# A causal pooling mixer reordered: group matrix product ahead of the token averages, averages as a banded matrix on TensorE

## The chip, the cores and the metric

The kernel runs on one core of a Trainium2 chip. The metric is the device time of one execution in microseconds; of several runs the median stands. A profile is of one execution.

## What is computed

The model has two layers on a stream x of 256 tokens by 2048 features, all in float32. Layer 0 mixes tokens by causal averages (the pooling mixer), layer 1 by latent attention; each is followed by a SwiGLU feed-forward part. The change is in the pooling mixer, the first thing the kernel does.

```python
def multiscale_pool_mixer(h, pool_w, pool_scale):      # h = rms_norm(x, pool_norm)
    cs = jnp.cumsum(hf, axis=1)
    for g, w in enumerate((2, 4, 8, 16)):              # a window for each group of 512 features
        c = cs[..., sl]
        c_prev = jnp.pad(c, ((0, 0), (w, 0), (0, 0)))[:, :S]
        count = jnp.minimum(t + 1, w)
        diff = (c - c_prev) / count - hf[..., sl]      # mean of the last w tokens, less the token itself
        outs.append(diff @ pool_w[g])                  # 512x512 matrix of the group
    return jnp.concatenate(outs, axis=-1) * pool_scale
x = x + multiscale_pool_mixer(rms_norm(x, pool_norm), pool_w, pool_scale)
x = x + (silu(h @ w_gate) * (h @ w_up)) @ w_down       # h = rms_norm(x, ffn_norm)
```

## The kernel before

Features lie on the 128 partitions, tokens along the free dimension: `x` is 16 tiles of 128x256, and tiles 4g to 4g+3 are group g. The engines run programs of their own and meet at semaphores; every order below is written out by hand.

**SyncE** issues all loads in one queue (`load`, L298 to L304): the four quarters of x (512 KB each), gains, constants, positions, and then eight chunks of `pool_w` of 512 KB into the eight slots of `raw`. After these come the chunks of the feed-forward weights (`up0`, ...), each as soon as the chunk that held its slot has been used.

**The pooling stage.** ScalarE squares the quarters of x into `x_square` (L710), VectorE adds them up (L1061, L1062), TensorE sums over the partitions with a matrix of ones (L424), ScalarE takes the root (L695) and VectorE the reciprocal (L1025, 128x256). ScalarE has meanwhile put x times the gain into `normed` (L715). VectorE multiplies by the reciprocal (L1072), makes the window sums of groups 0, 1 and 2 by shifted additions (L1080), corrects the first tokens (L1089) and writes mean less token into `pooled` (L1090). GpSimd does the multiplication of groups 1 to 3 (L1457) and the window sums of group 3 (L1448). TensorE then multiplies in float32 (`pool_tile`, L435): for each of 16 output tiles four matmuls with a 128x128 block of `raw` as the stationary operand and 256 columns of `pooled` as the moving one. The profile shows a float32 matmul as two records. VectorE adds the product to x (`pool_out`, L1099).

**The hand-over.** Each finished tile of x goes through `gained`: ScalarE writes the rounded product with the next gain (L701), VectorE the rest (L1031), side by side in `xg` as float32r. ScalarE also squares the tile (L724), and GpSimd adds it to `square_sum` (L1509). The first four weight chunks of `up0` are split in the same manner, high part by ScalarE (L689), low part by GpSimd (L1502); all later low parts are VectorE's (L1021).

**The feed-forward part** starts with `first_tiles`: two output tiles side by side, over tiles 0 to 7 of `xg` with chunks 0 and 1, then over tiles 8 to 15 with chunks 2 and 3. A product is a pair: `w_hi` on 512 columns (L373) and `w_lo` on 256 columns (L374). Then comes `sum_over_partitions` (L414) and the rest of the kernel, which the change leaves as it is.

## Time and profile before

| | |
|---|---|
| median of 3 runs | 1820.53 us (1820.5 to 1821.93) |
| span of the profiled execution, first to last instruction | 1818.9 us |
| TensorE busy | 1774.5 us, 98% |
| VectorE busy | 1163.2 us, 64% |
| ScalarE busy | 921.5 us, 51% |
| GpSimd busy | 188.2 us, 10% |
| first matmul of the feed-forward part starts | 67.44 us |
| `sum_over_partitions` after `first_tiles` starts | 78.62 us |

Of the profiled execution only the span is on record; the median of the runs is 1.6 us above it. Times within the trace count from the start of the span. PE is TensorE, PEld its loads of the stationary operand, DVE VectorE, ACT ScalarE, POOL GpSimd, SP SyncE. "ps" is the accumulator memory (PSUM), eight banks of 512 columns. Rows that name L701 and L724 (ScalarE) are a tile's hand-over.

### The profile page before, as it was taken

The numbers are of one execution on the slowest core, as the hardware profiler recorded it, in microseconds if no ns is written. First come the engines' busy times: TensorE is split into PE (matmuls) and PEld (weight loads), VectorE is DVE, ScalarE is ACT, GpSimd is POOL, SyncE is SP. The second block draws the span as 40 slices with busy tenths as digits, with TensorE's granted clock in tenths as the row PEclk, the third lists the DMA queues.
The fourth block names the chain that finished last, engine by engine and source line by source line (L and its number), as shares of the span: only waits on it lengthen the run. The fifth ranks groups of instructions, "written<-read, shape, count | busy, mean of one in ns | idle before, by whom it ended". The sixth has DMA issues, their size and how long they took to land.

```text
span 1818.9 us, 29323 instructions
## 1 busy us (share of the span) xinstructions
PE 1774.5 (98%) x10300; PEld 1571.6 (86%) x10300; DVE 1163.2 (64%) x1427; ACT 921.5 (51%) x1195; POOL 188.2 (10%) x198
## 2 busy tenths in 40 slices
PE   6899999999999999999999999999999999999997
PEld 5788888888888888888888888888888888888886
DVE  7766666556666666668777776666655566666554
ACT  3565655333445454456776456556533344445442
POOL 5400000000000001124322430000000000000112
PEclk8999999999999999999999999999999999999998
DMA  4555556654555565544334556555655455556541
GB/s 180 172 196 189 184 188 230 201 177 153 192 187 190 190 231 192 178 150 134 122 127 139 195 175 197 192 188 190 229 198 181 150 188 192 186 192 225 194 162 46
DMA packets 83998, 326.64 MB, mean 180 GB/s; under 512 B 9456, under 2 KB 9712, under 8 KB 83952
## 3 DMA queue, kind: packets, MB, share of 16 engines
q1 hardware_dynamic: 83952, 326.04, 54.2%
q8 instruction: 27, 0.44, 0.1%
q14 instruction: 19, 0.16, 0.0%
HBM read 323.91 MB, written 2.10 MB: 179 GB/s over the span
## 4 chain that ended last, share of the span: by engine, by line
PE 90%; DVE 5%; ACT 3%; issue 2%; POOL 0%; DMA 0%; DVEq 0%; SPq 0%; ACTq 0%; POOLq 0%
PE ps L373 57%; PE ps L374 30%; ACT w_hi L689 1%; DVE win_v L1080 1%; ACT product L845 1%; PE ps L435 0%; DVE xg L1031 0%; DVE w_lo L1021 0%; DMA x<-xT 0%; PE ps L527 0%; DVE prob L1355 0%; PE ps L526 0%; PE ps L525 0%; DVE pooled L1090 0%; ACT prob L905 0%
## 5 line engine op out<-in xcount | busy, mean ns | idle before, releaser
L1021 DVE TENSOR_TENSOR w_lo<-raw,w_hi 128x1024 fp32r<-128x1024 f32 (+2 forms) x557 | 731.3, 1315 | 422.6 <-ACT w_hi L689 422.1
L373 PE MATMUL ps<-xg,w_hi 128*128 128x512 f32 x2880 | 999.4, 390 | 1.0 <-POOL w_lo L1502 1.0
L689 ACT ACTIVATE w_hi<-raw 128x1024 fp32r<-128x1024 f32 (+2 forms) x562 | 630.2, 1124 | 494.5 <-PE ps L374 494.5
L374 PE MATMUL ps<-xg,w_lo 128*128 128x256 f32 x2880 | 812.2, 282 | 0.0
L373 PEld LDWEIGHTS ps<-xg,w_hi 128*128 128x128 f32 x2880 | 540.4, 188 | 114.7 <-POOL w_lo L1502 1.4
L374 PEld LDWEIGHTS ps<-xg,w_lo 128*128 128x128 f32 x2880 | 544.3, 189 | 0.1
L373 PE MATMUL ps<-act,w_hi 128*128 128x512 f32 x1408 | 488.3, 390 | 0.0
L374 PE MATMUL ps<-act,w_lo 128*128 128x256 f32 x1408 | 397.1, 282 | 0.0
L373 PEld LDWEIGHTS ps<-act,w_hi 128*128 128x128 f32 x1408 | 264.2, 188 | 55.4
L374 PEld LDWEIGHTS ps<-act,w_lo 128*128 128x128 f32 x1408 | 266.1, 189 | 0.0
L1467 POOL TENSOR_TENSOR square<-x 128x256 f32 (+1 forms) x47 | 42.4, 903 | 1452.0 <-DVE x L1151 1452.0
L1130 DVE TENSOR_TENSOR sums<-ps,cross 128x512 f32<-128x512 f32 x88 | 60.9, 692 | 95.6 <-ACT cross L734 95.6
L734 ACT ACTIVATE cross<-ps 128x512 f32<-128x512 f32 x88 | 52.6, 598 | 120.6 <-PE ps L374 120.5
L373 PE MATMUL ps<-heads,w_hi 128*128 128x512 f32 x256 | 89.1, 391 | 0.0
L1150 DVE TENSOR_TENSOR x<-ps,x 128x256 f32 (+1 forms) x80 | 33.8, 422 | 66.4 <-PE ps L374 66.4
L701 ACT ACTIVATE xg<-x,gain 128x256 fp32r<-128x256 f32 (+1 forms) x48 | 24.4, 508 | 100.4 <-DVE x L1151 62.1
L374 PE MATMUL ps<-heads,w_lo 128*128 128x256 f32 x256 | 72.2, 282 | 0.0
L1134 DVE TENSOR_TENSOR sums<-sums,rstd 128x512 f32<-128x512 f32 x88 | 60.9, 692 | 3.0
L737 ACT ACTIVATE gate_act<-sums 128x256 f32<-128x256 f32 x88 | 36.8, 418 | 46.0 <-DVE sums L1134 45.7
L373 PE MATMUL ps<-latent,w_hi 128*128 128x512 f32 x160 | 56.9, 395 | 0.6 <-DVE sums L1300 0.6
L373 PEld LDWEIGHTS ps<-heads,w_hi 128*128 128x128 f32 x256 | 48.1, 188 | 10.0
L1031 DVE SCALAR_TENSOR_TENSOR xg<-x,gain,xg 128x256 fp32r<-128x256 f32 (+1 forms) x48 | 39.4, 832 | 19.9 <-ACT xg L701 19.8
(168 smaller groups left out, 1202.5 us busy)
## 6 DMA issues: line engine op xcount, KB each, us to landing
raw<-w_gate SPq DMA_DIRECT2D x176, 512.0 KB, 3.5
raw<-w_up SPq DMA_DIRECT2D x176, 512.0 KB, 3.3
raw<-w_down SPq DMA_DIRECT2D x128, 704.0 KB, 4.1
raw<-w_o SPq DMA_DIRECT2D x32, 512.0 KB, 3.3
raw<-pool_w SPq DMA_DIRECT2D x8, 512.0 KB, 11.0
raw<-w_q_a SPq DMA_DIRECT2D x8, 512.0 KB, 3.3
raw<-w_kv_a SPq DMA_DIRECT2D x8, 512.0 KB, 3.3
raw<-w_q_nope SPq DMA_DIRECT2D x8, 512.0 KB, 3.3
```

Source lines behind the costliest of these rows:

```text
L373: pe.matmul(ps[:, bank, :], w_hi[:, s, j * P:(j + 1) * P], moving, start=start, stop=False)
L374: return pe.matmul(ps[:, bank, 0:SEQ], w_lo[:, s, j * P:(j + 1) * P], moving[:, 0:SEQ], start=False, stop=stop)
L689: nc.scalar.activation(dst, src, ACT.Copy).then_inc(hi_ready, 1)
L701: nc.scalar.activation(dst[:, plus(t, i, per), 0:SEQ], x[:, plus(t, i, per), :], ACT.Identity, scale=gain[:, plus(col + t, i, per), :]).th ...
L734: nc.scalar.activation(cross[:, :, :], ps[:, bank:bank + 2, SEQ:], ACT.Copy).then_inc(cross_ready, 1)
L737: nc.scalar.activation(gate_act[:, :], sums[:, 0, :], ACT.Silu).then_inc(gate_ready, 1)
L1021: nc.vector.tensor_tensor(lo, src, hi.bitcast(F32), ALU.subtract).then_inc(lo_ready, 1)
L1031: nc.vector.scalar_tensor_tensor(dst[:, plus(t, i, per), SEQ:], x[:, plus(t, i, per), :], gain[:, plus(col + t, i, per), :], dst[:, plus(t ...
L1130: nc.vector.tensor_tensor(sums[:, :, :], ps[:, bank:bank + 2, 0:SEQ], cross[:, :, :], ALU.add).then_inc(evacuated, 2)
L1134: nc.vector.tensor_tensor(sums[:, :, :], sums[:, :, :], r, ALU.mult).then_inc(sums_ready, 1)
L1150: step(nc.vector.tensor_tensor(xd, ps[:, b, 0:SEQ], xd, ALU.add))
L1467: step(nc.gpsimd.tensor_tensor(square[:, :], src, src, ALU.mult))
```

## The change

- TensorE multiplies by the group's matrix first (`pool_product`): the stationary operand is a block of `x_pool`, which is x times the gain with tokens as its 128 columns, the moving operand 512 columns of `raw`, in float32. The result has tokens on the partitions, 512 features of the group along the free dimension, in banks 4 to 7. A chunk of `pool_w` now holds half of a group's rows.
- The norm is applied to that result: a token is a partition there, so `tok_rstd` is a column of 128 for each half of the tokens. Squares are summed by `token_squares`, two columns wide; root and reciprocal are 128x2.
- ScalarE writes the scaled result rounded (`product_hi`), VectorE the rest (`product_lo`) into `z`, float32r.
- The averages are a banded 256x256 matrix for each window, made on the host and loaded as `bands` (128 partitions x 4 x 272 numbers, 544 KB). GpSimd brings it to float32r (`band`). `mix` multiplies `z` as the stationary operand by it: five matmuls a tile, of 256, 144, 16, 128 and 128 columns. The last group's `mix` stands in the middle of `first_tiles`.
- `pool_out` reads what `mix` left, and goes on with `gained` tile by tile or group by group. The low parts of the first four chunks of `up0` are VectorE's now.
- The loads are reordered: gains and `pool_w` chunks go between the quarters of x. The window sums, their corrections and buffers are gone, as are 18 matmuls of warm-up after the sum of squares; the first warm-up has 10 instead of 8. GpSimd's first fills have a 128x1600 one for `band` among them, for which the warm-up waits.

```diff
-WARM_UP = 8
-WARM_UP_POOL = 18
+WARM_UP = 10
...
+SPILL = P + PAD
+BAND_IN = SPILL + P
+B_FIRST, B_SECOND, B_LOW, B_COLS = 0, SEQ, SEQ + P, SEQ + P + PAD
...
+        z = at("z", [P, 2, 2, 2, GT * P], F32R, pool_at)
+        x_pool = at("x_pool", [P, DT, SEQ], F32, pool_at + 16 * KB)
+        band_in = at("band_in", [P, GROUPS, BAND_IN], F32, pool_at + 32 * KB)
+        band = at("band", [P, GROUPS, B_COLS], F32R, pool_at + 38 * KB)
+        tok_root = at("tok_root", [P, 2, 1], F32, scratch_at)
+        tok_rstd = at("tok_rstd", [P, 2, 1], F32, scratch_at + 64)
...
+        def mix_bank(t):
+            return t % GT if t < DT - GT else GT + t % GT
...
+            load_x(0)
+            sp.dma_start(gain[:, :, :], gains).then_inc(gain_landed, 16)
+            load(0, pool_w[0])
+            load_x(1)
+            load_x(2)
+            load(1, pool_w[1])
+            load_x(3)
+            load(2, pool_w[2])
+            sp.dma_start(band_in[:, :, :], bands).then_inc(band_landed, 16)
+            for c in range(3, 2 * GROUPS):
+                load(c, pool_w[c])
...
-                        bank_free(t + m)
+                        if t == TILE["up0"]:
+                            pe.wait_ge(evacuated, t + m - 7)
+                        else:
+                            bank_free(t + m)
...
-            for _ in range(WARM_UP_POOL):
-                pe.matmul(ps[:, SCORES, 0:P], ones[:, :], ones[:, :], start=True, stop=True)
...
+            def pool_product(g, half):
+                c = 2 * g + half
+                pe.wait_ge(landed[c], 16)
+                for s in range(2):
+                    if half == 0 and g >= 2:
+                        pe.wait_ge(z_ready, 2 * (g - 2) + s + 1)
+                    for j in range(2):
+                        kt = 2 * half + j
+                        if s == 0:
+                            pe.wait_ge(pool_gained, GT * g + kt + 1)
+                        mm = pe.matmul(ps[:, 4 + 2 * (g % 2) + s, :], x_pool[:, GT * g + kt, s * P:(s + 1) * P],
+                                       raw[:, c, j * GT * P:(j + 1) * GT * P], start=(kt == 0), stop=(kt == GT - 1))
+                mm.then_inc(chunks_used, 1)
+            def token_squares():
+                pe.wait_ge(quarter_ready, 4)
+                for s in range(2):
+                    mm = pe.matmul(ps[:, s, 0:2], x_square[:, DT - GT, s * P:(s + 1) * P], ones[:, 0:2],
+                                   start=True, stop=True)
+                mm.then_inc(stats_summed, 1)
+            def mix(g):
+                pe.wait_ge(z_ready, 2 * g + 2)
+                for j in range(GT):
+                    t = GT * g + j
+                    if 4 <= t < 12:
+                        pe.wait_ge(evacuated, t - 3)
+                    bank = mix_bank(t)
+                    first_hi, first_lo = (z[:, g % 2, 0, part, j * P:(j + 1) * P] for part in range(2))
+                    second_hi, second_lo = (z[:, g % 2, 1, part, j * P:(j + 1) * P] for part in range(2))
+                    pe.matmul(ps[:, bank, 0:SEQ], first_hi, band[:, g, B_FIRST:B_FIRST + SEQ], start=True, stop=False)
+                    pe.matmul(ps[:, bank, 0:SPILL], first_lo, band[:, g, B_FIRST:B_FIRST + SPILL], start=False,
+                              stop=False)
+                    pe.matmul(ps[:, bank, 0:PAD], first_hi, band[:, g, B_LOW:B_LOW + PAD], start=False, stop=False)
+                    pe.matmul(ps[:, bank, P:SEQ], second_hi, band[:, g, B_SECOND:B_SECOND + P], start=False,
+                              stop=False)
+                    pe.matmul(ps[:, bank, P:SEQ], second_lo, band[:, g, B_SECOND:B_SECOND + P], start=False,
+                              stop=True).then_inc(mixed, 1)
+            pool_product(0, 0)
+            pool_product(0, 1)
+            pool_product(1, 0)
+            token_squares()
+            pool_product(1, 1)
+            pe.wait_ge(band_ready, 3)
+            mix(0)
+            pool_product(2, 0)
+            pool_product(2, 1)
+            mix(1)
+            pool_product(3, 0)
+            pool_product(3, 1)
+            mix(2)
...
+                    if layer == 0:
+                        first_tiles(n0, t0, xg_before, (0,))
+                        mix(GROUPS - 1)
+                        first_tiles(n0, t0, xg_before, (1,))
+                    else:
+                        first_tiles(n0, t0, xg_before)
...
+            def product_hi(g):
+                sc.wait_ge(chunks_used, 2 * g + 2)
+                if g >= 2:
+                    sc.wait_ge(mixed, GT * (g - 1))
+                for s in range(2):
+                    nc.scalar.activation(z[:, g % 2, s, 0, :], ps[:, 4 + 2 * (g % 2) + s, :], ACT.Identity,
+                                         scale=tok_rstd[:, s, :]).then_inc(z_hi, 1)
...
+            def pooled_tile(t):
...
+            sc.wait_ge(gain_landed, 16)
+            pool_gain(0)
+            quarter_square(0)
+            pool_gain(1)
+            quarter_square(1)
+            quarter_square(2)
+            quarter_square(3)
+            pool_gain(2)
+            sc.wait_ge(stats_summed, 1)
+            nc.scalar.activation(tok_root[:, :, :], ps[:, 0:2, 0:1], ACT.Sqrt, bias=eps[:, :],
+                                 scale=1.0 / D_MODEL).then_inc(root_ready, 1)
+            sc.wait_ge(rstd_ready, 1)
+            product_hi(0)
+            pool_gain(3)
+            product_hi(1)
+            for t in range(4):
+                pooled_tile(t)
+            split(CHUNK["up0"])
+            product_hi(2)
+            for t in range(4, 8):
+                pooled_tile(t)
+            split(CHUNK["up0"] + 1)
+            product_hi(3)
+            for t in range(8, 12):
+                pooled_tile(t)
+            split(CHUNK["up0"] + 2)
+            split(CHUNK["up0"] + 3)
+            for t in range(12, DT):
+                pooled_tile(t)
...
-                nc.vector.tensor_tensor(c, c, x_square[:, 4 * q + 1, :], ALU.add).then_inc(quarter_ready, 1)
-            ve.wait_ge(init_ready, INIT)
-            ve.wait_ge(const_landed, 16)
+                ins = nc.vector.tensor_tensor(c, c, x_square[:, 4 * q + 1, :], ALU.add)
+                if q >= 1:
+                    step(ins)
+                    ins = nc.vector.tensor_tensor(c, c, x_square[:, 4 * q - 4, :], ALU.add)
+                ins.then_inc(quarter_ready, 1)
+                ve.wait_ge(quarter_ready, q + 1)
...
-            def pool_out(*tiles):
-                for t in tiles:
-                    if t % 2 == 0:
-                        ve.wait_ge(chunks_used, t // 2 + 1)
-                    nc.vector.scalar_tensor_tensor(x[:, t, :], ps[:, t % 4, 0:SEQ], gain[:, G_SCALE + t, :],
-                                                   x[:, t, :], ALU.mult, ALU.add).then_inc(evacuated, 1)
-            for a in (0, GT // 2):
-                b = a + GT // 2
-                norm_tiles(a, b, b)
-                pool_diff(0, window_sums(0, a, b), a // (GT // 2) + 1, a, b)
-            ve.wait_ge(normed_ready, 1)
-            pool_diff(1, window_sums(1), 3)
-            pool_out(0, 1, 2, 3)
-            ve.wait_ge(normed_ready, 2)
-            win = window_sums(2)
-            pool_out(4, 5)
-            pool_diff(2, win, 4)
-            pool_out(6, 7)
-            ve.wait_ge(windows_ready, 1)
-            pool_diff(3, win_p2, 5)
-            for t in range(DT // 2):
-                gained(t, G_FFN0, xg, t + 1)
-            for t in range(DT // 2, DT):
+            ve.wait_ge(root_ready, 1)
+            nc.vector.reciprocal(tok_rstd[:, :, :], tok_root[:, :, :]).then_inc(rstd_ready, 1)
+            ve.wait_ge(rstd_ready, 1)
+            def product_lo(g):
+                for s in range(2):
+                    ve.wait_ge(z_hi, 2 * g + s + 1)
+                    nc.vector.scalar_tensor_tensor(
+                        z[:, g % 2, s, 1, :], ps[:, 4 + 2 * (g % 2) + s, :], tok_rstd[:, s, :],
+                        z[:, g % 2, s, 0, :].bitcast(F32), ALU.mult, ALU.subtract).then_inc(z_ready, 1)
+            def pool_out(t):
+                ve.wait_ge(mixed, t + 1)
+                nc.vector.scalar_tensor_tensor(x[:, t, :], ps[:, mix_bank(t), 0:SEQ], gain[:, G_SCALE + t, :],
+                                               x[:, t, :], ALU.mult, ALU.add).then_inc(evacuated, 1)
+            product_lo(0)
+            product_lo(1)
...
+            for g in range(GROUPS - 1):
+                for t in range(GT * g, GT * g + GT):
+                    pool_out(t)
+                for t in range(GT * g, GT * g + GT):
+                    gained(t, G_FFN0, xg, t + 1)
+                split(CHUNK["up0"] + g)
+                if g < 2:
+                    product_lo(g + 2)
+            split(CHUNK["up0"] + GROUPS - 1)
+            for t in range(DT - GT, DT):
                 pool_out(t)
                 gained(t, G_FFN0, xg, t + 1)
-            ve.wait_ge(lo_ready, SPLIT_SLOTS)
...
+            for ap, value in ((ones[:, :], 1.0), (eps[:, :], EPS), (band[:, :, :].bitcast(F32), 0.0),
+                              (stat[:, :, :], 0.0)):
...
+            gp.wait_ge(band_landed, 16)
+            nc.gpsimd.tensor_copy(band[:, :, B_FIRST:B_FIRST + SPILL], band_in[:, :, 0:SPILL]).then_inc(band_ready, 1)
+            nc.gpsimd.tensor_copy(band[:, :, B_SECOND:B_SECOND + P], band_in[:, :, SPILL:]).then_inc(band_ready, 1)
+            gp.wait_ge(band_ready, 2)
+            nc.gpsimd.tensor_tensor(band[:, :, B_LOW:B_LOW + PAD], band_in[:, :, 0:PAD],
+                                    band[:, :, B_FIRST:B_FIRST + PAD].bitcast(F32), ALU.subtract).then_inc(band_ready, 1)
...
-                if t in FIRST_SPLITS:
-                    split(CHUNK["up0"] + FIRST_SPLITS.index(t))
...
+def pool_bands():
+    s, t = np.arange(P)[:, None], np.arange(SPILL)[None, :]
+    out = np.zeros((P, GROUPS, BAND_IN), np.float32)
+    for g, w in enumerate(WINDOWS):
+        seen, own = (t >= s) & (t < s + w), (t == s).astype(np.float32)
+        out[:, g, 0:SPILL] = np.where(seen, 1.0 / np.minimum(t + 1.0, w), 0.0) - own
+        out[:, g, SPILL:] = (np.where(seen, 1.0 / w, 0.0) - own)[:, 0:P]
+    return out
...
-        "pool_w": np.concatenate([by_tiles(w, GT, 2) for w in a["pool_w"][0]]),
+        "pool_w": a["pool_w"][0].reshape(2 * GROUPS, 2, P, GT * P).transpose(0, 2, 1, 3).reshape(2 * GROUPS, P, -1),
```

## Rows read from the trace of the kernel before

**Rows 1.** The page: the span and the busy time of each engine.
```profile
span 1818.9 us, 29323 instructions
...
PE 1774.5 (98%) x10300; PEld 1571.6 (86%) x10300; DVE 1163.2 (64%) x1427; ACT 921.5 (51%) x1195; POOL 188.2 (10%) x198
```

**Rows 2.** Windows: length, PE, PEld, DVE, ACT, POOL busy, PE's clock, DMA share, GB/s.
```profile
0.00:67.44 67.44, 47.02 (x188) 38.05 (x189) 54.23 (x53) 25.43 (x52) 41.32 (x36) 0.90 0.43 155
...
78.78:1818.90 1740.12, 1716.17 (x10048) 1523.52 (x10047) 1102.25 (x1364) 889.89 (x1133) 143.81 (x158) 1.00 0.55 180
```

**Rows 3.** The chain that ended last, 0 to 82 us: start, length, what.
```profile
13.58 1.76 DVE rstd L1025
...
37.74 8.85 PE ps L435 x32
...
66.68 0.77 issue
```

**Rows 4.** Timeline of PE: start, length, what, records.
```profile
1.66 3.79 PE L421 MATMUL ps<-ones 128*128 128x128 f32 x16 [1.66 <-POOL stat L1444]
...
37.74 15.74 PE L435 MATMUL ps<-pooled,raw 128*128 128x256 f32 x64 [2.96 <-DVE x L1099]
...
67.87 0.39 PE L373 MATMUL ps<-xg,w_hi 128*128 128x512 f32 x1
...
78.62 0.59 PE L414 MATMUL ps<-square_sum,ones 128*128 128x256 f32 x2
```

**Rows 5.** Windows in the pooling stage (columns as in rows 2).
```profile
23.90:27.50 3.60, 3.57 (x8) 2.86 (x9) 3.56 (x2) 0.00 (x0) 3.52 (x2) 0.50 0.00 0
27.50:29.50 2.00, 1.94 (x9) 1.38 (x7) 1.97 (x2) 0.00 (x0) 1.92 (x2) 0.98 0.00 0
```

**Rows 6.** Timeline of PE in the attention part, float32r matmuls back to back.
```profile
960.73 0.28 PE L596 MATMUL ps<-probT,v_buf 128*128 128x256 f32 x1
960.85 0.22 PE L594 MATMUL ps<-probT,v_buf 128*128 128x128 f32 x1
960.91 0.28 PE L595 MATMUL ps<-probT,v_buf 128*128 128x128 f32 x1
961.02 0.27 PE L596 MATMUL ps<-probT,v_buf 128*128 128x128 f32 x1
```

**Rows 7.** Timeline of POOL: fills, and one addition of the window sums.
```profile
0.74 0.20 POOL L1444 MEMSET ones<- 128x128 f32 x1 [0.29 <-POOLq L1623]
...
0.92 0.31 POOL L1444 MEMSET normed<- 128x256 f32 x1
...
23.40 2.22 POOL L1448 TENSOR_TENSOR win_p<-normed 128x1024 f32<-128x1024 f32 x1
```

**Rows 8.** Timeline of ACT at the start of the kernel.
```profile
5.11 1.06 ACT L710 ACTIVATE x_square<-x 128x1024 f32<-128x1024 f32 x1 [2.87 <-DMA x<-xT]
6.38 1.06 ACT L710 ACTIVATE x_square<-x 128x1024 f32<-128x1024 f32 x1 [0.22 <-DMA x<-xT]
...
13.35 4.88 ACT L715 ACTIVATE normed<-x,gain 128x256 f32<-128x256 f32 x12
```

**Rows 9.** Timeline of DVE.
```profile
10.51 0.69 DVE L1061 TENSOR_TENSOR x_square<-x_square 128x512 f32<-128x512 f32 x1
...
26.21 2.27 DVE L1080 TENSOR_TENSOR win_v<-normed 128x512 f32<-128x512 f32 x1
...
66.87 0.47 DVE L1099 SCALAR_TENSOR_TENSOR x<-ps,gain,x 128x256 f32<-128x256 f32 x1
...
68.33 0.47 DVE L1099 SCALAR_TENSOR_TENSOR x<-ps,gain,x 128x256 f32<-128x256 f32 x1
```

**Rows 10.** The page's groups: line, operation, count, busy, mean ns, idle before.
```profile
L1021 DVE TENSOR_TENSOR w_lo<-raw,w_hi 128x1024 fp32r<-128x1024 f32 (+2 forms) x557 | 731.3, 1315 | 422.6 <-ACT w_hi L689 422.1
...
L689 ACT ACTIVATE w_hi<-raw 128x1024 fp32r<-128x1024 f32 (+2 forms) x562 | 630.2, 1124 | 494.5 <-PE ps L374 494.5
...
L734 ACT ACTIVATE cross<-ps 128x512 f32<-128x512 f32 x88 | 52.6, 598 | 120.6 <-PE ps L374 120.5
```

More of the change, by code:

```diff
@@ L133, in plus, with trunk @@
     return n if i is None else i * per + n
-def trunk(nc, xT, positions, consts, gains, pool_w, w_kv_a, w_k_pe, w_q_a, w_kv_k, w_kv_v, w_q_nope, w_q_pe,
+def trunk(nc, xT, positions, consts, bands, gains, pool_w, w_kv_a, w_k_pe, w_q_a, w_kv_k, w_kv_v, w_q_nope, w_q_pe,
           w_o, w_gate, w_up, w_down, out):
@@ L246, in trunk @@
         init_ready = sem("init_ready")
-        windows_ready = sem("windows_ready")
-        normed_ready = sem("normed_ready")
-        diff_ready = sem("diff_ready")
+        band_landed = sem("band_landed")
+        band_ready = sem("band_ready")
+        z_hi = sem("z_hi")
+        z_ready = sem("z_ready")
+        mixed = sem("mixed")
         angle_ready = sem("angle_ready")
@@ L289, in trunk @@
         KV, Q = 0, 1
-        INIT = 8
+        INIT = 4
         UPS = ("up0", "up1", "up2", "up3")
@@ L304, in load, with load_x @@
                 sp.dma_start(raw[:, n % WEIGHT_SLOTS, 0:chunk_elems(n)], src).then_inc(landed[n % WEIGHT_SLOTS], 16)
-            for q in range(4):
+            def load_x(q):
                 sp.dma_start(x[:, 4 * q:4 * q + 4, :], xT[:, 4 * q:4 * q + 4, :]).then_inc(x_landed[q], 16)
-                if q == 1:
-                    sp.dma_start(gain[:, :, :], gains).then_inc(gain_landed, 16)
+            load_x(0)
[9 more added lines that the diff above has]
+                load(c, pool_w[c])
             sp.dma_start(const[:, :], consts).then_inc(const_landed, 16)
             sp.dma_start(pos_i[:, :], positions.partition_broadcast(P)).then_inc(pos_landed, 16)
-            for c in range(CHUNK["up0"]):
-                load(CHUNK["pool"] + c, pool_w[c])
             def ffn(layer, half):
@@ L421, in _ @@
                 pe.matmul(ps[:, SCORES, 0:P], ones[:, :], ones[:, :], start=True, stop=True)
-            for q in range(4):
-                pe.wait_ge(quarter_ready, q + 1)
-                mm = pe.matmul(ps[:, STATS, 0:SEQ], ones[:, :], x_square[:, 4 * q, :], start=(q == 0), stop=(q == 3))
-            mm.then_inc(stats_summed, 1)
-            for _ in range(WARM_UP_POOL):
-                pe.matmul(ps[:, SCORES, 0:P], ones[:, :], ones[:, :], start=True, stop=True)
-            def pool_tile(t, kts):
-                c = t // 2
-                for kt in kts:
-                    j = t % 2 * GT + kt
-                    mm = pe.matmul(ps[:, t % 4, 0:SEQ], raw[:, c, j * P:(j + 1) * P], pooled[:, c // 2 * GT + kt, :],
-                                   start=(kt == 0), stop=(kt == GT - 1))
-                if t % 2 == 1 and kts[-1] == GT - 1:
-                    mm.then_inc(chunks_used, 1)
@@ L441, in _ @@
-            for part in range(2):
-                pe.wait_ge(diff_ready, part + 1)
-                for t in range(GT):
-                    if part == 0 and t % 2 == 0:
-                        pe.wait_ge(landed[t // 2], 16)
-                    pool_tile(t, range(part * GT // 2, (part + 1) * GT // 2))
-            for t in range(GT, DT):
-                if t % GT == 0:
-                    pe.wait_ge(diff_ready, t // GT + 2)
-                if t % 2 == 0:
-                    pe.wait_ge(landed[t // 2], 16)
-                bank_free(t)
-                pool_tile(t, range(GT))
+            def pool_product(g, half):
[11 more added lines that the diff above has]
+                mm.then_inc(chunks_used, 1)
@@ L706, in _, with pool_gain, quarter_square @@
             nc.scalar.activation(stat[:, 0, 7:8], eps[:, :], ACT.Sqrt)
-            for q in range(4):
+            def pool_gain(q):
+                sc.wait_ge(x_landed[q], 16)
+                for t in range(GT * q, GT * q + GT):
+                    nc.scalar.activation(x_pool[:, t, :], x[:, t, :], ACT.Identity,
+                                         scale=gain[:, G_POOL + t, :]).then_inc(pool_gained, 1)
+            def quarter_square(q):
                 sc.wait_ge(x_landed[q], 16)
@@ L711, in _ @@
                                      ACT.Square).then_inc(squares_ready, 1)
-            sc.wait_ge(gain_landed, 16)
-            for t in range(DT):
-                nc.scalar.activation(normed[:, t, PAD:], x[:, t, :], ACT.Identity,
-                                     scale=gain[:, G_POOL + t, :]).then_inc(pool_gained, 1)
-                if t == GT - 1:
-                    root_of(1, D_MODEL)
-            for t in range(DT):
+            def product_hi(g):
[6 more added lines that the diff above has]
+            def pooled_tile(t):
                 gained(t, TILE["pool"] + t + 1, G_FFN0, xg)
@@ L1603 @@
         "consts": shape_constants(),
+        "bands": pool_bands(),
         "gains": np.concatenate([feature_tiles(v.reshape(-1)) for v in (
```

63 lines of the change are left out of this document (6 added, 57 removed).

## The prediction

> **What bounds the kernel now.** I began with the page's busy times. TensorE is busy for 1774.5 of 1818.9 us, so 44 us are all that it idles [rows 1]. The windows say where: up to the first feed-forward matmul at 67.44 us it works 47.0 of 67.4 us, a gap of 20.4 us; from 78.78 us to the end it works 1716.2 of 1740.1 us [rows 2]. That second part can't be helped by this change, and it will simply start earlier if the first part ends earlier. The chain of waits shows why the first part is long: it goes through VectorE's reciprocal of 128x256 (1.76 us), the window sums, and then a TensorE that multiplies in short bursts; the last wait is 0.77 us ahead of the first feed-forward matmul [rows 3]. So the question is when `first_tiles` ends. Before, `sum_over_partitions` starts right behind it at 78.62 us [rows 4]; call the same moment after the change E. The time moves by E minus 78.6.
>
> **Prices on TensorE.** The second half of the 64 records of the old float32 products takes 15.74 - 8.85 = 6.89 us, so 0.215 us a record of 256 columns and 0.43 us a matmul [rows 3, 4]. That is at the full granted clock; in the first burst the clock is at 0.50 for 3.6 us, with 8 records there (0.45 us each), and then 0.98 [rows 5]. A new product has 512 moving columns. No row shows a float32 matmul so wide. The lower bound is twice 0.43 = 0.86 us; the upper one twice the half-clock price, 1.78 us. I take 0.86, since TensorE is to run without long gaps here. Half a group (4 matmuls) is then 3.44 us and all eight are 27.6 us, exactly what the 64 old ones cost at full clock: the reorder saves TensorE nothing, it moves its work ahead.
>
> `mix` is added: 80 float32r matmuls. Back to back, 256 columns take 0.12 us and 128 columns mostly 0.11, once 0.06 [rows 6]. I take 0.12 + 4 x 0.11 = 0.57 us a tile (also for the 16 and 144 columns), 2.3 us a group; the lower bound is 0.12 + 4 x 0.06 = 0.36 us. By the Trainium skill, "TensorE: Matmul & The Clock Gate", section "Back-to-back issue gap", spacing follows the columns (about 60 cycles up to 64 columns, 134 at 128, 262 at 256), so that a tile would be an estimated 0.31 us; its section "LDWEIGHTS" gives columns / 1.2 GHz for the stationary operand, 107 ns for 128 columns, and the 0.11 us of the trace agrees with that one.
>
> A pair of the feed-forward part is (78.62 - 67.87) / 31 = 0.347 us [rows 4].
>
> **The start.** The fill of `band` is new. 128 more columns cost 0.11 us (0.20 to 0.31 [rows 7]), so 1600 columns take 1.5 us, and the warm-up starts at 2.5 instead of 1.66 us. Its 20 records at 3.79 / 16 = 0.237 us [rows 4] end at 7.2. Loads: quarter 0 of x lands at 5.1 us and the next 1.27 us later [rows 8], 512 KB each. In the new order that gives chunk 0 of `pool_w` at 6.4 to 6.9 (with the gains ahead), x at 8.1 and 9.4, chunk 1 at 10.7, x at 12.0, chunk 2 at 13.2, `bands` (544 KB) at 14.6, chunk 3 at 15.9, the last at 21.0. ScalarE makes a 128x256 tile in 4.88 / 12 = 0.41 us and a quarter's squares in 1.06 [rows 8]: gain 0 until 7.3, then squares 0 at 8.3, gain 1 at 9.9, squares 1 to 3 at 11.0, 12.0 and 13.1, gain 2 at 14.7. VectorE needs 1.6 us a quarter (0.69 + twice 0.42) and is through at 15.8.
>
> **The ladder of TensorE**, each step at the price above:
> - product (0,0) 7.2 to 10.7; (0,1) to 14.1; (1,0) to 17.6, each chunk landed in time
> - `token_squares`: 4 short records at 0.11, 0.5, to 18.1; its sums have been ready since 15.8
> - product (1,1) to 21.5. Beneath it run the root (18.8), a 128x2 reciprocal instead of 1.76 us (19.0), two ScalarE passes of 0.60 [rows 10] to 20.2 and VectorE's rest, 0.69 each, to 20.9. That hides the norm; without this cover it would cost 2.8 us
> - `mix` 0 to 23.8; group 2's products to 30.7; `mix` 1 to 33.0; group 3's to 39.9; `mix` 2 to 42.2
> - the first feed-forward matmul wants bank 0 back, so tile 8 in x. VectorE has first `product_lo` 3 (ScalarE from 39.9, VectorE done at 42.0), then 0.44: 42.5
> - 16 pairs, 5.55, to 48.1; `mix` 3 to 50.4
> - the second half waits for the last four tiles. ScalarE hands tiles 8 to 11 over until 45.8 and splits two chunks at 1.12 [rows 10] until 48.0; VectorE's low part of the last ends at 49.5 (1.3 each [rows 10]). Then a tile takes 68.33 - 66.87 = 1.46 us, pool_out, ScalarE, VectorE in turn [rows 9]. The sixteenth is there at 49.5 + 4 x 1.46 = 55.3; its pair and eight more end at 58.5.
>
> The window sums, `normed`'s multiplications and the second warm-up go with their whole cost, none of it replaced on VectorE. The tile hand-overs stay, but twelve of sixteen lie beneath TensorE's work. VectorE between 21 and 49.5 us has three `product_lo` (4.2), twelve `pool_out` (5), twelve rests (5) and four splits (5.2): 19.4 of 28.5 us. The four low parts of `up0` move from POOL to VectorE at 1.3 instead of 2.4 us, and are hidden up to the last two. The loads of `up0` queue behind `pool_w` on SyncE and wait for products that end at 10.7, 14.1 and so on, far ahead of their use at 28; the constants now come after `pool_w` and are first needed in the feed-forward part.
>
> E = 58.5, so 20.1 us less. I take off 0.6 for a clock that may rise only within the first product and for the start-up of TensorE after its waits: 19.5 us. The span becomes 1799.4 and, since the median stood 1.6 above the profiled span, the median 1801.0.
>
> **What rows say of VectorE and POOL together.** The same addition of 512 columns takes 0.69 us alone and 2.27 us while POOL adds windows [rows 9]. After the change POOL has the band's conversion (1152 columns; at 2.22 us for 1024 at most 2.5 us [rows 7]), about 14.6 to 17.1 us, across VectorE's last square sums, and 16 additions of 0.7 us. So squares may be ready at 18.3 instead of 15.8: 0.7 us on the ladder. The Trainium skill, "SBUF — State Buffer", section "SBUF: two separate sides", says that a VectorE instruction with two SBUF inputs and a reading POOL instruction exclude each other for whole instructions. The trace agrees (0.69 against 2.27 us). By that rule the sum grows by no more than POOL's own work.
>
> **Rivals.**
> 1. *The other engines set the pace.* VectorE's 19.4 us grow by up to POOL's 9 us beneath them (twelve additions) to 28.4, and the hand-over with ScalarE adds its waits. Then `mix` or the feed-forward part waits for evacuations. Against it: 9 us of slack. Price 4 to 6 us: about 1806.
> 2. *Low clock.* The first burst of before shows 3.6 us at 0.50 [rows 5]. If two half groups run so, 2 x 3.6 = 7.1 us: 1808.
> 3. *Short matmuls are cheap.* At 0.36 us a tile, the lower bound [rows 6], twelve tiles ahead of the last chain give 12 x 0.21 = 2.5 us: 1798.5. (By the page cited above, "TensorE: Matmul & The Clock Gate" of the Trainium skill, it would be an estimated 3.2 us.)
> 4. *Slower than before.* A float32 matmul of 512 columns costs 1.78 us everywhere, by a clock that stays down or a surcharge on wide operands. 32 x 0.92 = 29.4 us, more than the 20 gained: 1830. It decides from 0.86 + 20 / 32 = 1.48 us a matmul. For it: no row of such a matmul. Against: the feed-forward pairs with 512 columns cost in proportion.
> 5. *It doesn't carry through*: the weights' stream or ScalarE holds the feed-forward part, and the gain is waited away: 1820. Against: TensorE at 98.6% with DMA at 0.55 [rows 2].
>
> **How the numbers follow.** Forecast 0.60, rival 1 0.18, rival 2 0.08, rival 3 0.08, rival 4 0.04, rival 5 0.02. A difference under 0.2% (3.6 us) can't be told from none. Faster 0.94, same 0.02, slower 0.04. The range goes from rival 3 to rival 2, 1797.5 to 1808.
>
> **What would show it.** Right: the first float32r pair of the feed-forward part near 42.5 us, `sum_over_partitions` near 58.5, TensorE without a gap over 1 us from 7 us until `mix` 3, 0.86 us a product matmul, 0.57 us a mixed tile, and the rest from there as long as before (1740 us). Wrong: gaps ahead of `mix` 0 (the norm isn't hidden), ahead of `mix` 2 or the first pair (rival 1), records of 0.4 us and more in the products (rivals 2, 4), or a second part longer than 1740 us (rival 5).

## The result and the profile after

The changed kernel takes 1803.28 us (median of 4 runs, 1801.16 to 1804.13) against 1820.74 us: 17.5 us less. The ratio is 0.9899, 95% interval 0.9887 to 0.9911. The forecast was 1801.0 us, with a range of 1797.5 to 1808. The profiled execution has a span of 1802.3 us and took 1804.13 us itself, the slowest of the four; the fastest took 1801.16.

The page, and windows at three places: up to the first pair of the feed-forward part, up to `sum_over_partitions`, and the rest. Columns as in [rows 1, 2].

```profile
span 1802.3 us, 29277 instructions
...
PE 1773.5 (98%) x10280; PEld 1562.5 (87%) x10280; DVE 1140.1 (63%) x1423; ACT 925.1 (51%) x1203; POOL 160.1 (9%) x186
```

```profile
0.00:43.49 43.49, 40.07 (x148) 23.94 (x149) 24.79 (x40) 25.14 (x50) 10.11 (x20) 1.00 0.72 265
43.49:60.86 17.37, 15.66 (x84) 13.28 (x85) 13.86 (x20) 10.89 (x21) 6.10 (x8) 0.90 0.45 148
60.86:1802.30 1741.44, 1717.81 (x10050) 1525.26 (x10048) 1101.50 (x1364) 889.08 (x1133) 143.89 (x158) 1.00 0.54 180
```

TensorE now idles 3.4 us ahead of the first pair, where it idled 20.4 us before [rows 2]. The first pair is at 43.5 instead of 67.4 us, `sum_over_partitions` at 60.86 instead of 78.62 [rows 4]: 17.8 us. The rest takes 1741.4 us; before it was 1818.9 - 78.62 = 1740.3. The two account for the 16.6 us between the spans.

TensorE's timeline, start and length. It answers to [rows 4, 6].

```profile
2.46 4.64 PE L438 MATMUL ps<-ones 128*128 128x128 f32 x20 [2.46 <-POOL stat L1501]
7.55 11.15 PE L451 MATMUL ps<-raw,x_pool 128*128 128x512 f32 x24 [0.46 <-DMA raw<-pool_w]
18.53 0.50 PE L459 MATMUL ps<-ones,x_square 128*128 128x2 f32 x4
18.90 3.68 PE L451 MATMUL ps<-raw,x_pool 128*128 128x512 f32 x8
...
23.49 0.34 PE L473 MATMUL ps<-band,z 128*128 128x256 f32 x1
23.66 0.23 PE L474 MATMUL ps<-band,z 128*128 128x144 f32 x1
23.73 0.22 PE L476 MATMUL ps<-band,z 128*128 128x16 f32 x1
23.80 0.31 PE L477 MATMUL ps<-band,z 128*128 128x128 f32 x1
23.95 0.28 PE L479 MATMUL ps<-band,z 128*128 128x128 f32 x1
24.06 0.33 PE L473 MATMUL ps<-band,z 128*128 128x256 f32 x1
...
24.62 7.08 PE L451 MATMUL ps<-raw,x_pool 128*128 128x512 f32 x16
...
33.75 7.08 PE L451 MATMUL ps<-raw,x_pool 128*128 128x512 f32 x16
...
43.49 0.47 PE L386 MATMUL ps<-xg,w_hi 128*128 128x512 f32 x1 [0.46 <-issue]
...
56.22 0.80 PE L386 MATMUL ps<-xg,w_hi 128*128 128x512 f32 x1 [0.84 <-DVE xg L1113]
...
57.02 0.63 PE L386 MATMUL ps<-xg,w_hi 128*128 128x512 f32 x1
...
57.67 0.63 PE L386 MATMUL ps<-xg,w_hi 128*128 128x512 f32 x1
...
60.86 0.59 PE L432 MATMUL ps<-square_sum,ones 128*128 128x256 f32 x2
```

From 7.5 us on TensorE works almost without a gap. A mixed tile starts 0.57 us after the one before it (23.49 to 24.06). From one group's products to the next 9.13 us pass (24.62 to 33.75); less four mixed tiles that is 6.85 us for eight matmuls (16 records), 0.43 us a record. From 56.22 us a pair costs 0.65 instead of 0.35 us, though nothing is waited for there. VectorE's timeline over group 2 and the end of the stage, for [rows 9]:

```profile
32.46 1.41 DVE L1159 SCALAR_TENSOR_TENSOR z<-ps,tok_rstd,z 128x512 fp32r<-128x512 f32 x2 [1.58 <-ACT z L771]
...
41.59 1.41 DVE L1159 SCALAR_TENSOR_TENSOR z<-ps,tok_rstd,z 128x512 fp32r<-128x512 f32 x2 [1.58 <-ACT z L771]
42.92 1.65 DVE L1165 SCALAR_TENSOR_TENSOR x<-ps,gain,x 128x256 f32<-128x256 f32 x4
44.48 3.58 DVE L1113 SCALAR_TENSOR_TENSOR xg<-x,gain,xg 128x256 fp32r<-128x256 f32 x4
47.99 2.35 DVE L1103 TENSOR_TENSOR w_lo<-raw,w_hi 128x1024 fp32r<-128x1024 f32 x2
50.26 0.47 DVE L1165 SCALAR_TENSOR_TENSOR x<-ps,gain,x 128x256 f32<-128x256 f32 x1
...
55.68 0.48 DVE L1113 SCALAR_TENSOR_TENSOR xg<-x,gain,xg 128x256 fp32r<-128x256 f32 x1 [0.58 <-ACT xg L747]
```

The wait of 1.58 us comes once a group: VectorE has that much to spare. The four rests of a group take 3.58 us, 0.9 each. The last four tiles go in turn, and the sixteenth is ready at 55.68 + 0.48 = 56.2 us.

### The profile page after: what moved, and what is told of

The parts are those of the page before. It is cut to its first block, busy times and chain, and to the rows that moved or that the text cites. A ratio compares the mean times of both kernels' runs of the same rounds, so it can differ in the third digit from the quotient of the medians.

```text
span 1802.3 us, 29277 instructions
## 1 busy us (share of the span) xinstructions
PE 1773.5 (98%) x10280; PEld 1562.5 (87%) x10280; DVE 1140.1 (63%) x1423; ACT 925.1 (51%) x1203; POOL 160.1 (9%) x186
## 4 chain that ended last, share of the span: by engine, by line
PE 92%; DVE 3%; ACT 2%; issue 1%; DMA 0%; POOL 0%; DVEq 0%; SPq 0%; ACTq 0%
PE ps L386 58%; PE ps L387 31%; PE ps L451 1%; ACT product L927 1%; DMA raw<-pool_w 0%; ACT w_hi L735 0%; DVE w_lo L1103 0%; PE ps L572 0%; PE ps L573 0%; PE ps L571 0%; DVE prob L1413 0%; ACT prob L987 0%; ACT prob L989 0%; DVE xg L1113 0%; PE ps L621 0%
## 5 line engine op out<-in xcount | busy, mean ns | idle before, releaser
L1514 POOL TENSOR_TENSOR square<-x 128x256 f32 (+1 forms) x47 | 42.5, 904 | 1452.0 <-DVE x L1208 1452.0
```

Of the source, the lines that this page charges most:

```text
L1514: step(nc.gpsimd.tensor_tensor(square[:, :], src, src, ALU.mult))
```

## The experiments

"Fourth product" is TensorE's second one of group 1, at 18.90 us above. This start varies by some 2 us from one execution to the next: with the same program up to there it lies at 18.73 (e9), 18.90 (e2), 19.02 (e7), 19.19 (e6), 19.38 (e11), 20.43 (e5) and 20.55 us (e1). The two late ones began their products slowly:

```profile
8.05 12.30 PE L451 MATMUL ps<-raw,x_pool 128*128 128x512 f32 x24 [0.96 <-DMA raw<-pool_w]
7.60 12.63 PE L451 MATMUL ps<-raw,x_pool 128*128 128x512 f32 x24 [0.51 <-DMA raw<-pool_w]
```

The first line is of e1, the second of e5. At 0.43 us, 24 records take 10.3 us. In both the loads of the stationary operand start 0.86 us apart until about 11.7 us and 0.43 us apart from there, though the granted clock is given as 1.00 for that stretch. So where the end of the stage is the question, times are counted from that mark: in the changed kernel the sixteenth tile comes 37.3 us behind it and `sum_over_partitions` 42.0.

| kernel | median us | before, same chip | sixteenth tile | sum_over_partitions |
|---|---|---|---|---|
| changed | 1803.28 | 1820.74 | +37.3 | +42.0 |
| e1, two passes | 1802.44 | 1820.69 | +36.5 | +39.8 |
| e2, fillers | 1801.49 | 1820.69 | +37.3 | +40.6 |
| e3, norm first | 1813.08 | 1820.69 | | (70.87 us) |
| e4, old loads | 1808.74 | 1820.69 | +37.3 | +40.6 |
| e5, 6 more on VectorE | 1804.25 (one run) | 1820.89 | +37.3 | +40.6 |
| e6, 12 more | 1805.73 (one run) | 1820.89 | +41.3 | +44.6 |
| e7, mix 3 early | 1803.67 | 1820.89 | +37.2 | +42.0 |
| e8, before with fillers | 1820.71 | 1820.89 | | (78.34 us) |
| e9, squares behind | 1800.55 | 1821.06 | +35.2 | +39.4 |
| e10, in all groups | 1800.87 | 1821.06 | +35.5 | +38.8 |
| e11, short mix | 1800.94 | 1821.06 | +34.6 | +39.5 |

**e3: how much is the matrix ahead of the norm?**

```diff
-            pool_product(0, 0)
-            pool_product(0, 1)
-            pool_product(1, 0)
             token_squares()
+            pool_product(0, 0)
+            pool_product(0, 1)
+            pool_product(1, 0)
             pool_product(1, 1)
```

> The changed kernel, with token_squares ahead of the first product, so that TensorE starts the group matrices only when the sum of squares is there (17.0 us in the profile of the changed kernel), as the kernel before did. Theory: what the change gains comes first of all from TensorE's 28 us of products starting before the norm is known. Then everything from the first product on moves from 7.55 to about 17.4 us and, as the second product had waited for its chunk until 11.5 us, the rest moves by 9.3 us: sum_over_partitions at about 70, the span about 9 us longer, half of the gain gone. Rival: the stage is set by VectorE's and ScalarE's work, then 0 to 4 us.

TensorE of e3:

```profile
17.31 1.01 PE L459 MATMUL ps<-ones,x_square 128*128 128x2 f32 x4 [10.22 <-DVE x_square L1147]
18.19 15.80 PE L451 MATMUL ps<-raw,x_pool 128*128 128x512 f32 x32
```

The median is 9.8 us above that of the changed kernel, 1813.08 to 1803.28; 9.3 were expected. In the profiles the sixteenth tile is 11.4 us later (67.6 instead of 56.2 us). Of these, 1.9 us are not the late start alone: after its wait of 10 us TensorE began the products with records 0.86 us apart, so that 32 of them took 15.80 instead of 13.9 us. On the other hand, the profile of e3 has neither of the two falls of the clock that cost the changed kernel 1.4 and 1.2 us (below). So of 17.5 us some 10, the slow records included, come from TensorE's start ahead of the norm, and with that taken away the kernel is still 7.6 us faster than before.

**e8: was it only the clock?** The old stage had three stretches of half clock.

```diff
-WARM_UP_POOL = 18
+WARM_UP_POOL = 40
...
+                if t in (GT, 3 * GT):
+                    for _ in range(9 if t == GT else 13):
+                        pe.matmul(ps[:, SCORES, 0:P], ones[:, :], ones[:, :], start=True, stop=True)
                 if t % GT == 0:
                     pe.wait_ge(diff_ready, t // GT + 2)
```

> The kernel before, with short matmuls of ones in TensorE's waits of the pooling stage (22 more behind the sum of squares, 9 ahead of group 1, 13 ahead of group 3). Nothing else is moved. Rival explanation of the gain: TensorE's low clock in the old stage (three stretches of 3.4 us at 0.50) cost most of it, and the reorder only keeps the clock up; then this kernel gains 5 us. Theory: only the burst from 37.7 us lies on the path, so the gain is 1.7 us, up to 3.4 if the burst from 57.6 counts too, and the other 14 us are the order of the work.

Timeline of TensorE and windows of e8:

```profile
39.21 13.98 PE L435 MATMUL ps<-pooled,raw 128*128 128x256 f32 x64
...
57.27 3.69 PE L435 MATMUL ps<-pooled,raw 128*128 128x256 f32 x16 [1.19 <-DVE x L1102]
62.24 3.69 PE L435 MATMUL ps<-pooled,raw 128*128 128x256 f32 x16 [1.27 <-DVE x L1102]
...
78.34 0.59 PE L414 MATMUL ps<-square_sum,ones 128*128 128x256 f32 x2
```

```profile
31.00:34.40 3.40, 3.40 (x9) 2.68 (x10) 3.37 (x2) 0.00 (x0) 2.14 (x2) 0.50 0.00 0
...
37.70:41.00 3.30, 3.30 (x24) 3.09 (x24) 3.27 (x4) 2.54 (x8) 2.58 (x3) 1.00 0.48 159
...
57.00:62.00 5.00, 3.69 (x16) 2.96 (x16) 3.65 (x5) 2.47 (x5) 3.66 (x3) 1.00 0.00 0
```

From 37.7 us on the clock is at 1.00, and the last 32 records take twice 3.69 us instead of 8.83. Still `sum_over_partitions` starts at 78.34 instead of 78.62, and the time is the same (ratio 1.0001, 0.9991 to 1.0010). Both theories expected too much. For the last 32 records the case is clear: faster by far, and nothing moved. For the burst from 37.7 us it is mixed: the fillers did not remove a low clock but moved it, to the burst ahead (16 records from 30.75 us took 6.62 us where they took 3.72 before), and this burst and the fillers pushed the next start back by 1.5 us (39.21 against 37.74). Its 64 records then took 13.98 instead of 15.74 us; the two cancel. So e8 alone doesn't settle this burst. The trace of before does:

```profile
46.68 0.88 DVE L1099 SCALAR_TENSOR_TENSOR x<-ps,gain,x 128x256 f32<-128x256 f32 x2 [0.65 <-PE ps L435]
```

In the whole old stage this is VectorE's only wait for TensorE's products, so not more than 0.65 us could have been won there. Not the clock but VectorE, with its window sums and rests, held the old stage.

**e5, e6: does VectorE set the pace now?** N is 6 and 12. Each was executed once, so the times at the mark count here.

```diff
                 split(CHUNK["up0"] + g)
+                if g == 0:
+                    for _ in range(N):
+                        step(nc.vector.scalar_tensor_tensor(rstd[:, :], x[:, 0, :], gain[:, G_SCALE, :], x[:, 1, :],
+                                                            ALU.mult, ALU.add))
```

> The changed kernel with 6 more VectorE instructions of 0.42 us each (2.5 us, their result is read by nobody) behind the hand-over of group 0. Theory: VectorE has about 3.2 us of idle time in groups 1 and 2 (two waits of 1.6 us for ScalarE), so 2.5 us are absorbed: sum_over_partitions within 0.3 us of 60.9. Rival (VectorE sets the pace of the stage): 2.5 us later.

> The same with 12 such instructions (5.0 us). Theory: 3.2 us absorbed, the rest moves the evacuation of tile 8, the first feed-forward pair and the tail by 1.8 us. Rival (VectorE sets the pace): 5 us later.

The twelve of e6 took 6.20 us, 0.52 each with the step between them:

```profile
31.10 6.20 DVE L1178 SCALAR_TENSOR_TENSOR rstd<-x,gain 128x256 f32<-128x256 f32 x12
```

In e5 some 3.1 us vanish to the last tenth (+37.3 as without). Of the 6.2 in e6, 3.2 should be absorbed and 3.0 be left; the first pair is at 46.71, 27.5 behind the fourth product instead of 24.6, so 2.9 later. The sixteenth tile is some 4 us later: behind TensorE's wait of 3.39 us the granted clock was at 0.52 (46.7 to 50.0 us), the first five pairs cost 0.64 us each, and the last group's `mix` behind them came so late that VectorE waited 1.08 us for it. The slack of two times 1.58 us was read rightly from the profile.

**e11: does TensorE's ladder set it?** Two of the five matmuls of `mix` are left, 256 and 128 columns.

```diff
-                    pe.matmul(ps[:, bank, 0:SPILL], first_lo, band[:, g, B_FIRST:B_FIRST + SPILL], start=False,
-                              stop=False)
-                    pe.matmul(ps[:, bank, 0:PAD], first_hi, band[:, g, B_LOW:B_LOW + PAD], start=False, stop=False)
                     pe.matmul(ps[:, bank, P:SEQ], second_hi, band[:, g, B_SECOND:B_SECOND + P], start=False,
-                              stop=False)
-                    pe.matmul(ps[:, bank, P:SEQ], second_lo, band[:, g, B_SECOND:B_SECOND + P], start=False,
                               stop=True).then_inc(mixed, 1)
```

> The changed kernel with only two of the five matmuls of mix (the low parts and the correction are left out, so the averages are those of rounded numbers). A mixed tile costs 0.28 instead of 0.57 us on TensorE. Theory: TensorE's ladder sets when group 3's product is there, two mixes (8 tiles) lie ahead of it, so it and the tail come 2.3 us earlier, sum_over_partitions too. Rival (VectorE sets the pace of the groups): less than 0.5 us.

The sixteenth tile comes 2.7 us earlier, the median is 2.3 lower. A mixed tile cost 0.23 us and not 0.28, and the 0.34 us saved on each of eight tiles are these 2.7 us. VectorE's wait ahead of `product_lo` 3 shrinks from 1.58 to 0.25 us:

```profile
39.39 1.41 DVE L1154 SCALAR_TENSOR_TENSOR z<-ps,tok_rstd,z 128x512 fp32r<-128x512 f32 x2 [0.25 <-ACT z L766]
```

TensorE in turn now waits 1.80 us ahead of the first pair, instead of 0.46. So TensorE sets the pace of the groups, but VectorE is close behind.

**e2: the clock at the end of the stage.**

```diff
                         if m == 0:
+                            if t == TILE["up0"] and kt > DT - GT:
+                                for _ in range(3):
+                                    pe.matmul(ps[:, 2, 0:P], ones[:, :], ones[:, :], start=True, stop=True)
                             pe.wait_ge(xg_ready, xg_before + kt + 1)
```

> The changed kernel, with three short float32 matmuls of ones (into a bank that is free) ahead of each of TensorE's waits for the last three tiles of xg. Nothing else is moved. Theory: the pairs from 56.2 to 59.2 us cost 0.64 instead of 0.35 us because the clock fell to 0.50 while TensorE waited for tiles; with the engine kept at work they cost 0.35 us and sum_over_partitions starts 1.3 to 1.4 us earlier, the sixteenth tile is ready when it was. Rival: the clock falls by something else, then the fillers cost their own time, up to 0.7 us.

Window of the changed kernel, then that of e2 over the same pairs:

```profile
56.20:59.20 3.00, 2.98 (x9) 2.60 (x10) 2.27 (x2) 2.59 (x3) 0.62 (x1) 0.50 0.00 0
```

```profile
56.20:59.40 3.20, 3.17 (x18) 2.81 (x19) 2.46 (x3) 2.61 (x3) 0.63 (x1) 1.00 0.00 0
```

`sum_over_partitions` starts 1.4 us earlier, the sixteenth tile when it did. In e3, e4, e5 and e6 the clock held without fillers and `sum_over_partitions` comes 3.3 us behind the sixteenth tile instead of 4.7. The work of the tail is the same in all of them, so whether the clock falls there seems to differ from one execution to the next; each kernel has one profile only.

**e1, e9, e10: the last tiles.** e1 takes them in two passes:

```diff
             for t in range(DT - GT, DT):
                 pool_out(t)
+            for t in range(DT - GT, DT):
                 gained(t, G_FFN0, xg, t + 1)
```

> The changed kernel, with the four last tiles taken in two passes on VectorE (pool_out for tiles 12 to 15, then gained for 12 to 15) instead of in turn. Theory: the end of the stage is set by the hand-over in turn, 1.46 us a tile, and TensorE idles between its pairs there until its granted clock falls to 0.50. Then the sixteenth tile of xg is ready at about 53.9 instead of 56.2 us, the clock stays at 1.00, sum_over_partitions starts at about 57.0 instead of 60.9 us, and the time falls by 3.5 to 4 us. If only the wait counts and the clock falls anyway: 2.3 us. Rival: TensorE's own ladder (products and mix) sets the end, then nothing moves.

The end came 2.2 us earlier, but 1.4 of them are the clock, which held; the hand-over itself gained 0.8 instead of 2.3 us. VectorE's four rests took 3.45 us in e1. e9 puts ScalarE's squares behind its high parts, so that GpSimd adds later:

```diff
+            def pooled_tiles(first):
+                for t in range(first, first + GT):
+                    gained(t, TILE["pool"] + t + 1, G_FFN0, xg)
+                for t in range(first, first + GT):
+                    if t >= 4:
+                        sc.wait_ge(squares_added, t - 3)
+                    nc.scalar.activation(square_of(t), x[:, t, :], ACT.Square).then_inc(square_made, 1)
...
-            for t in range(12, DT):
-                pooled_tile(t)
+            pooled_tiles(12)
```

> The kernel of e1 (last four tiles in two passes), and ScalarE takes the four high parts of xg first and the four squares behind them. Theory: in e1 VectorE's four rests took 0.86 us each instead of the 0.42 to 0.48 of one alone because GpSimd's additions of the squares ran between them and both read SBUF; with the squares behind, the rests have no addition beside them, take 0.42 to 0.48 us each, and the sixteenth tile is ready 1.7 us earlier than in e1, sum_over_partitions too (counted from the start of the fourth product: 38.1 instead of 39.8 us). Rival: the rests wait for ScalarE, then they come 0.41 us apart all the same but only 0.6 us are gained; or GpSimd's additions, now later, hold sum_over_partitions, then nothing is gained.

VectorE of e1 and of e9, then GpSimd of e9:

```profile
53.59 3.45 DVE L1113 SCALAR_TENSOR_TENSOR xg<-x,gain,xg 128x256 fp32r<-128x256 f32 x4
```

```profile
51.77 2.16 DVE L1120 SCALAR_TENSOR_TENSOR xg<-x,gain,xg 128x256 fp32r<-128x256 f32 x4
54.61 4.57 DVE L1110 TENSOR_TENSOR w_lo<-raw,w_hi 128x1024 fp32r<-128x1024 f32 x3 [0.69 <-ACT w_hi L735]
```

```profile
54.61 3.49 POOL L1564 TENSOR_TENSOR square_sum<-square_sum,sums 128x256 f32<-128x256 f32 x2
```

Three of the four rests take 0.48 us, the fourth 0.97: GpSimd's first addition starts at 52.85 us, just ahead of it. In e1, with additions beside them, they take 0.82 to 0.95 us. The sixteenth tile gains another 1.3 instead of the expected 1.7 us. But the additions now meet VectorE's splits, two of them take 3.49 us, and TensorE waits 0.78 us for the sum: only 0.3 us are left at `sum_over_partitions`. The second rival of e9 held in part. e10 does so in all groups and loads the second chunk earlier:

> The kernel of e9 with the same order (four high parts, then four squares) in all four groups, and the second chunk of pool_w ahead of the third quarter of x. Theory: in the inner groups VectorE's rests shrink from 3.5 to about 1.7 us, but VectorE has idle time there and the splits wait for ScalarE; the tail starts 0.4 us earlier. The second product starts 0.4 us earlier. Against e9: 0.8 us. Rival: the splits' low parts now meet GpSimd's additions, then nothing or 0.5 us worse.

Another 0.6 us at the mark's count, none in the median (1800.87 and 1800.55). The second product did come 0.4 us earlier. The rests shrank to 2.15 us in every group, but the tail did not start earlier: the additions, moved behind them, met the splits, as the rival had it. Two splits took 3.45 us where they took 2.35, and the sixteenth tile is 0.3 us later than in e9.

```profile
46.82 3.45 DVE L1107 TENSOR_TENSOR w_lo<-raw,w_hi 128x1024 fp32r<-128x1024 f32 x2 [0.72 <-ACT w_hi L735]
```

What is gained at `sum_over_partitions` is the wait of 0.78 us that e9 had there. e9 and e10 are the fastest full kernels, 20.5 and 20.2 us below before; against the changed kernel's median they are 2.7 and 2.4 us lower, but that one was measured at another time, with 1820.74 us for the kernel before beside it instead of 1821.06.

**e4 and e7: loads, and the place of the last mix.** e4 loads all of x, gains, constants and positions ahead of `pool_w`; e7 is this:

```diff
-                        first_tiles(n0, t0, xg_before, (0,))
                         mix(GROUPS - 1)
-                        first_tiles(n0, t0, xg_before, (1,))
+                        first_tiles(n0, t0, xg_before)
```

> The changed kernel with the old order of the loads: all of x, constants and positions, then pool_w (bands behind its third chunk). Theory: the ladder hangs on the landing of the second chunk of pool_w and on nothing else early on; by 512 KB in 1.27 us the first chunk lands at 11.5 and the first product starts at 11.6 instead of 7.55 us, the second starts at 15.2 instead of 11.6, and the end of the stage moves by 3.6 us. Rival: the start is hidden behind later waits (the hand-over of the last tiles), then less than 1 us.

> The changed kernel with the last group's mix ahead of first_tiles instead of in its middle. Theory: the tail hangs on VectorE's order (it takes tile 12 only after two weight splits, at 50.3 us), so mixing group 3 some 6 us earlier doesn't make the sixteenth tile earlier; TensorE runs its first half 2.3 us later and waits less before the tail. Sum_over_partitions within 0.5 us of 60.9, up to 1.4 us earlier if the clock now holds. Rival: the place of that mix matters, TensorE is the limit, then 2.3 us later.

e4 is 5.5 us slower than the changed kernel; 3.6 were expected. Its first product starts at 12.80 instead of 11.6 us. Behind TensorE's wait of 6.32 us the granted clock was at 0.55 (12.8 to 16.3 us), and the first 24 records took 12.11 instead of 11.15 us; the fourth product starts at 25.11, 6.2 later. The reorder of the loads is worth about a third of the gain, and it overlaps with what e3 took away. e7 changes nothing, as expected.

## Why the prediction was right, and where it was off

**The ladder held.** Predicted and measured: first product 7.2 and 7.5, `mix` 0 at 21.5 and 22.6 (in the chain), first pair 42.5 and 43.5, sixteenth tile 55.3 and 56.2. The price of a float32 matmul of 512 columns was taken at its lower bound, 0.86 us, and is that; rival 4 is out. The mixed tile is 0.57 us as summed, though not by parts (below); rival 3 is out. The norm lay hidden under product (1,1) as said.

**Off by 0.9 us: the loads.** Chunk 1 landed at 11.5 instead of 10.7 us, so it was not there in time, and this is nearly all of the ladder's delay. The loads ahead of it were late already: chunk 0 at 7.5 instead of 6.9, x's second quarter at 8.9 instead of 8.1, its last at 13.1 instead of 12.0.

```profile
8.87 1.71 ACT L757 ACTIVATE x_pool<-x,gain 128x256 f32<-128x256 f32 x4 [0.46 <-DMA x<-xT]
...
13.13 1.06 ACT L762 ACTIVATE x_square<-x 128x1024 f32<-128x1024 f32 x1 [0.67 <-DMA x<-xT]
```

So 512 KB in 1.27 us behind a first landing at 5.1 was too fast for the first 13 us; why is open.

**Part of the closeness is luck.** The profiled execution began its products at full pace. In e1 and e5, whose program is the same up to there, the slow first records (rival 2's mechanism, for one half group) put the fourth product 1.5 to 1.7 us later, more than the 0.6 us taken off for such things.

**Mis-sized: VectorE's rests.** "Twelve rests (5)" were 10.6 us (3.52, 3.52 and 3.58), since each met one of GpSimd's additions. The prediction had the exclusion [rows 9] and gave it to rival 1 as 9 us of POOL's work; 5.6 us came. In groups 0 and 1 they fell into idle time, as e5 and e6 show. In group 2 they did not, for the chain that ended last runs through the rests and the two splits behind them, up to tile 12:

```profile
44.57 3.50 DVE xg L1113 x4
48.07 2.27 DVE w_lo L1103 x2
```

With rests of 0.42 us the first split could have begun when ScalarE's was done, at 47.3, and tile 12 at some 49.7 instead of 50.3 us: an estimated 0.6 us. It didn't show in the sum because ScalarE, which the prediction had ahead of tile 12, was done with its splits 0.5 us earlier than laid out (29.4 us behind the fourth product instead of 48.0 - 18.1 = 29.9), and because the prediction's 49.5 has 0.2 us more than its own 48.0 + 1.3. So rival 1 was right in kind and small. By the Trainium skill, "SBUF — State Buffer", section "SBUF: two separate sides", a VectorE instruction with two SBUF inputs and a GpSimd instruction that reads SBUF wait for each other whole; e9 agrees, with 0.48 us for a rest alone and 0.97 for the one that met an addition.

**Missed: the clock at the end.** The prediction looked for a low clock at the start (rival 2) and not at the tail, where it itself had TensorE wait 1.1 us between pairs. That fall cost 1.4 us in the profiled execution (e2). A second one came in the attention part; windows of the changed kernel and, over the same work, of the one before:

```profile
861.70:865.10 3.40, 3.40 (x19) 3.40 (x18) 1.89 (x3) 2.57 (x6) 0.85 (x1) 0.53 0.24 77
```

```profile
879.50:882.90 3.40, 3.40 (x32) 3.40 (x31) 1.89 (x3) 2.57 (x6) 0.89 (x1) 1.00 0.32 77
```

19 matmul records instead of 32 in 3.4 us. The rest of the kernel took 1.2 us longer for it: from `sum_over_partitions` on the profiles of the changed kernel, e4, e5, e7 and e10, which have the fall, take 1741.4 to 1741.5 us, those of before, e1, e2, e3, e6, e9 and e11, which have none, 1740.1 to 1740.3. The program is the same from there on, so I take the fall for chance of an execution and not for work of the change; the old kernel's two profiles, without it, are too few to show that it has it as often.

**The sum.** Of 2.9 us between the spans (1799.4 and 1802.3), 0.9 are the loads' delay of the ladder, 1.4 the clock at the tail, 1.2 the rest of the kernel; 0.6 allowed beforehand go off. This is an account of the profiled execution, the slowest of four; the median run has no trace. The fastest, 1801.16 us, lies on the forecast.

**Where the gain comes from.** The prediction gave no shares. Ten of 17.5 us hang on TensorE's products running ahead of the norm (e3); the rest I put down to what was taken from VectorE, whose work set the old stage while the clock did not (e8). That latter part rests on exclusion; no run moved the window sums alone. One share of it has not been separated: GpSimd's window sums slowed VectorE's work. Both lines are corrections of first tokens in the kernel before, the shorter one beside GpSimd's multiplications, the longer one when GpSimd was done:

```profile
18.86 2.21 DVE L1089 TENSOR_TENSOR win_v<-win_v,const 128x32 f32<-128x32 f32 x1
...
35.59 0.23 DVE L1089 TENSOR_TENSOR win_v<-win_v,const 128x64 f32<-128x64 f32 x1
```

So part of this gain may come from taking GpSimd's work from beside VectorE, and not from taking VectorE's own.

## What to carry to other kernels

Where a scale or an average commutes with a matrix product, put the product first: TensorE then works while the statistics are made, and here it paid even with 80 matmuls more, since what counts is the chain and not the sum. Lay out each engine's program as a ladder with the time of each rung and look for waits of TensorE near a microsecond behind each other at its end: besides their own length they can cost its clock. Moving one engine's work from beside another's only helps if it meets nothing at its new place (e9, e10). Before speeding up a stage that shows a low clock, check that TensorE is on its path at all.

## What the runs showed of the hardware

- A float32r matmul's time isn't set by its own columns alone: 256 columns take 0.12 us behind one of 256 (49.12 to 49.24) and 0.17 behind one of 128 (49.63 to 49.80). In a mixed tile the starts lie 0.17, 0.07, 0.07, 0.15 and 0.11 us apart for 256, 144, 16, 128 and 128 columns. The 16 columns cost 0.07 us, and the first 128 columns behind them 0.15. Only the sum, 0.57 us, is what the row of 0.11 us for 128 columns promised.
- The clock fell at the tail in the profiles of the changed kernel, e7 and e11 and held in those of e3, e4, e5 and e6, with the same pairs and waits of 0.72 to 0.84 us there.
- The column of the granted clock can miss a slow stretch: in e1, e3 and e5 the first records of the products started 0.86 us apart and later ones 0.43, and it reads 1.00 for both.
- A conversion of 576 columns to float32r took GpSimd 0.66 us and one of 512 columns 0.81 us; an addition of 1024 columns had taken 2.22 [rows 7]. Times on GpSimd are rough.
